# RWKV tile products on all four quarters of the array, the right factor of the inverse as a transpose of the left, and merge's first weights split ahead of its norm

## The reference, cut to what matters

```python
h = rmsnorm(x, p['norm_mix_g'])
u = h @ p['w_in']
o_ssd, ... = ssd_mixer(u_ssd, ...)       # ends with a grouped RMS norm of y
o_rwkv, ... = rwkv_mixer(u_rwkv, ...)
o_mla = attend(...)
gates = jax.nn.sigmoid(h @ p['w_gate'] + p['b_gate'])
merged = gates[0]*(o_ssd @ w_o_ssd) + gates[1]*(o_rwkv @ w_o_rwkv) + gates[2]*(o_mla @ w_o_mla)
x = x + merged @ p['w_out']
```

```python
def step(s, inp):
    r_t, w_t, k_t, v_t, kk_t, a_t = inp
    sa = jnp.einsum('bhvk,bhk->bhv', s, -kk_t)
    s = (s * w_t[:, :, None, :] + sa[..., None] * (kk_t * a_t)[:, :, None, :]
         + v_t[..., None] * k_t[:, :, None, :])
    return s, jnp.einsum('bhvk,bhk->bhv', s, r_t)
```

## Time and profile before

| | us |
|---|---|
| median of 3 executions | 3179.81 |
| lowest and highest of them | 3179.19, 3187.45 |
| the profiled execution | 3192.04 |
| its span in the profile | 3190.2 |
| TensorE busy | 2879.2 (90% of the span) |
| VectorE, ACT, POOL busy | 1796.7, 1349.2, 840.5 |
| stage `rwkv_tiles`, layer 0: first matmul to last DMA issue | 167.5 to 302.43 |
| stage `merge`, layer 0: squares to first unit | 1153.08 to 1169.06 |

### The profile page before, as it was taken

How to read it: one execution, slowest core, us unless ns; L and a number is a source line. 1 busy time by engine, 2 the same in 40 slices (tenths; PEclk the granted TensorE clock), 3 DMA queues, 4 the chain that set the end, 5 groups by cost and what they waited for, 6 DMA issues and landing times. The chain is left out here.

```text
span 3190.2 us, 66465 instructions
## 1 busy us (share of the span) xinstructions
PE 2879.2 (90%) x26560; PEld 2647.9 (83%) x26560; DVE 1796.7 (56%) x3035; ACT 1349.2 (42%) x2168; POOL 840.5 (26%) x696
## 2 busy tenths in 40 slices
PE   7888878999997889999978988789999978898998
PEld 6888547999997769989977984489999976798998
DVE  4843454555655645489448444545566556454893
ACT  4612343544544333254365133444454443333542
POOL 0030000699990400000000300008999804000000
PEclk9999988999998979999989999789999989899999
DMA  5301202212115266365453021022111152664544
GB/s 135 91 5 46 78 10 70 67 40 58 37 34 162 70 165 171 94 176 142 124 120 81 4 75 48 11 75 63 53 48 36 50 157 77 171 166 111 159 138 121
DMA packets 471247, 282.15 MB, mean 88 GB/s; under 512 B 65294, under 2 KB 466488, under 8 KB 470314
## 3 DMA queue, kind: packets, MB, share of 16 engines
q1 hardware_dynamic: 468724, 276.85, 31.4%
q10 hardware_dynamic: 2232, 1.26, 0.2%
HBM read 258.75 MB, written 19.29 MB: 87 GB/s over the span
## 5 line engine op out<-in xcount | busy, mean ns | idle before, releaser
L1112 PE MATMUL key_banks<-w_kb_head,latent_T_head 128*128 128x352 f32 x1536 | 518.4, 337 | 0.0
L1112 PE MATMUL key_banks<-w_kb_rest,latent_T_head 128*128 128x352 f32 x1536 | 496.6, 323 | 0.0
L1112 PE MATMUL key_banks<-w_kb_head,latent_T_rest 128*128 128x352 f32 x1536 | 496.0, 323 | 0.0
L290 DVE TENSOR_TENSOR w_rests<-w_ring,w_heads 128x2048 fp32r<-128x2048 f32 (+1 forms) x152 | 326.2, 2150 | 148.8 <-ACT w_heads L284 148.6
L931 POOL TENSOR_TENSOR rwkv_state_tmp<-rwkv_state,vec 128x1024 f32<-128x1024 f32 x64 | 153.1, 2392 | 683.9 <-DMA rwkv_state<-in_state_rwkv_dram 679.0
L1257 DVE TENSOR_REDUCE w_kb<-key_sq 128x8 f32<-128x1024 f32 x256 | 309.5, 1209 | 0.0
L1172 ACT CAST latent_T_head<-turn_bank 128x256 fp32r<-128x256 f32 x256 | 95.5, 373 | 477.2 <-PE turn_bank L1090 285.0
L284 ACT CAST w_heads<-w_ring 128x2048 fp32r<-128x2048 f32 (+1 forms) x152 | 271.9, 1793 | 51.5 <-ACT conv_last_rows L1795 19.7
L2663 POOL TENSOR_TENSOR L_level<-L,const 128x1024 f32<-128x1024 f32 x24 | 56.0, 2354 | 901.9 <-DVE L L2669 826.5
L1112 PEld LDWEIGHTS key_banks<-w_kb_rest,latent_T_head 128*128 128x128 f32 x1536 | 291.0, 189 | 0.0
L1112 PEld LDWEIGHTS key_banks<-w_kb_head,latent_T_head 128*128 128x128 f32 x1536 | 290.3, 189 | 0.0
(11 more groups left out here) (565 smaller groups left out, 7401.5 us busy)
## 6 DMA issues: line engine op xcount, KB each, us to landing
w_ring<-in_ffn_w_up_dram SPq DMA_DIRECT2D x88, 512.0 KB, 5.1
latents<-in_cache_kv_latent_dram SPq DMA_DIRECT2D x256, 128.0 KB, 2.0
w_ring<-in_w_in_dram SPq DMA_DIRECT2D x52, 512.0 KB, 3.8
w_ring<-in_w_gate_dram SPq DMA_DIRECT2D x48, 512.0 KB, 3.9
w_ring<-in_w_in_dram SPq DMA_DIRECT2D x20, 1024.0 KB, 6.2
w_ring<-in_ffn_w_down_dram SPq DMA_DIRECT2D x32, 384.0 KB, 3.6
w_ring<-in_ffn_w_down_dram SPq DMA_DIRECT2D x32, 320.0 KB, 4.1
rope_keys<-in_cache_k_rope_dram SPq DMA_DIRECT2D x256, 32.0 KB, 1.8
```

Source lines behind the costliest of these rows:

```text
L290: ops.tensor_tensor(rests[:, slot, 0:tiles * P], ring[:, slot, 0:tiles * P], heads[:, slot, 0:tiles * P].bitcast(F32), ALU.subtract).then_ ...
L1112: last = nc.tensor.matmul(kbank[:, 3 * x + n, 0:KB], c[:, x, r * P:(r + 1) * P], w[:, r, cols], start=r == 0 and m == 0, stop=r == 1 and m ...
```

## The change

**In `rwkv_tiles`** the address rules, the order, the inverse and the tail change.

- Quarters: a new `token_half(c, p)` is `p ^ (c & 1)`. Values with tokens on the partitions of an odd chunk are now kept on the other half. A product that goes from features to tokens, or from tokens to features (`to_tokens`, `to_features`, and `by_head(X)` by `by_head(Z)`), reads one half and writes the other where the chunk is odd, so that the 32 matmuls of a group use four quarters of the array in turn (`quads`). A product from tokens to tokens (`in_tokens`: `kav`, the first `z`, `ta`, `tk`) stays on the two quarters that it had, and so do `advance` and the new `from_state`. Of the 62 products of a group, 54 are now on four quarters.
- Inverse: X is no longer updated by Z X and an addition. After each level TensorE turns Y (`const,Y`), and the result is copied into X by VectorE (group 0) and ACT (group 1). POOL's masks no longer wait for X.
- Order: `l` comes first; `bend` and `kend` come ahead of the loop, and `z` and the turn of Y are issued by group.
- Tail: for the chunks 1 and 3 the product of R with the state is a matmul pass of its own (`from_state`), which VectorE adds to the output. The states' bank pair is 6 instead of 4.

**In `merge`** ACT's `w_heads` of units 0 and 1 and `out_heads` of the RWKV branch come ahead of `Ln` and `Exp`, and VectorE's `w_rests` and `out_rests` of the same come ahead of the 8 scalings.

```diff
+                heads_of(0)
+                nc.scalar.copy(oh[:, 0, :, :], branches[0][1][:, :, :]).then_inc(out_rounded, 1)
+                heads_of(1)
...
-                heads_of(0)
-                heads_of(1)
...
+                rests_of(0)
+                dve.wait_ge(out_rounded, 1)
+                nc.vector.tensor_tensor(ol[:, 0, :, :], branches[0][1][:, :, :], oh[:, 0, :, :].bitcast(F32), ALU.subtract).then_inc(out_split, 1)
+                rests_of(1)
...
-                rests_of(0)
-                rests_of(1)
...
-        def both(g):
-
-            for swap in range(2):
-                for t in range(DT):
-                    yield (2 * g + swap, t, 0), (2 * g + 1 - swap, t, 1)
+        st_out, y_added = st.sem("state_stored"), st.sem("y_from_state_added")
+
+        def feature_half(c, p):
+            return p
+
+        def token_half(c, p):
+            return p ^ (c & 1)
+
+        def quads(g):
+
+            for t in range(DT):
+                yield (2 * g, t, 0), (2 * g + 1, t, 0), (2 * g + 1, t, 1), (2 * g, t, 1)
...
         def by_token(buf):
+            return lambda c, t, p: buf[rows(token_half(c, p)), c, t * 64:(t + 1) * 64]
...
+                def multiply(g, slot, lhs, rhs, written):
+                    for quad in quads(g):
+                        for c, t, p in quad:
+                            last = nc.tensor.matmul(out(slot, c, t, written(c, p)), lhs(c, t, p), rhs(c, t, p),
+                                                    start=True, stop=True, skip_group_check=True)
                     return last
...
+                pe.wait_ge(kept["kav"], 2)
+                to_tokens(0, 1, k.kendT, feature_eye).then_inc(made["kend"], 1)
+                pe.wait_ge(kept["bend"], 2)
+                to_tokens(1, 3, k.kendT, feature_eye).then_inc(made["kend"], 1)
+                for g in range(2):
                     pe.wait_ge(level_in, g + 1)
-                    multiply(g, 2 + g, by_token(Ln), eye).then_inc(made["z"], 1)
+                    in_tokens(g, 2 * g, Ln, token_eye).then_inc(made["z"], 1)
                 for n in range(1, 6):
-                    z0 = 0 if n % 2 else 2
                     for g in range(2):
                         pe.wait_ge(level_in, 2 * n + g + 1)
                         pe.wait_ge(kept["y_inv"], 2 * (n - 1) + g + 1)
                         if n == 1:
-                            pe.wait_ge(kept["alpha"], g + 1)
-                        elif g:
-                            pe.wait_ge(kept["x_inv"], 2 * (n - 1) + 1)
-                        multiply(g, z0 + g, by_token(Ln), by_token(Y)).then_inc(made["z"], 1)
+                            pe.wait_ge(kept["kend"], g + 1)
+                        to_features(g, 2 * g + n % 2, Ln, by_token(Y)).then_inc(made["z"], 1)
+                        to_features(g, 2 * g + (n - 1) % 2, Y, token_eye).then_inc(made["x"], 1)
                     for g in range(2):
                         pe.wait_ge(kept["z"], 2 * (n - 1) + g + 1)
-                        pe.wait_ge(kept["x_inv"], 2 * (n - 1) + 2)
-                        pe.wait_ge(kept["y_inv"], 2 * (n - 1) + 2)
-                        slot = z0 if g else 2 - z0
-                        multiply(g, slot, by_token(X), by_token(Z)).then_inc(made["y_inv"], 1)
-                        if n < 5:
-                            if g:
-                                pe.wait_ge(kept["z"], 2 * (n - 1) + 2)
-                            multiply(g, slot + 1, by_token(Z), by_token(X)).then_inc(made["x_inv"], 1)
-                pe.wait_ge(kept["x_inv"], 10)
-                multiply(0, 3, by_feature(k.bendT), eye).then_inc(made["bend"], 1)
-                multiply(1, 1, by_feature(k.bendT), eye).then_inc(made["bend"], 1)
+                        pe.wait_ge(x_kept[g], n)
+                        multiply(g, 2 * g + (n - 1) % 2, by_head(X), by_head(Z), token_half).then_inc(made["y_inv"], 1)
                 for g in range(2):
                     pe.wait_ge(kept["y_inv"], 10 + g + 1)
-                    multiply(g, 2 - 2 * g, by_token(Y), by_token(alpha_tm)).then_inc(made["ta"], 1)
-                    pe.wait_ge(kept["bend"], g + 1)
-                    multiply(g, 3 - 2 * g, by_token(Y), by_token(kav)).then_inc(made["tk"], 1)
-                for g in range(2):
-                    pe.wait_ge(kept["ta"], g + 1)
-                    multiply(g, 2 - 2 * g, by_feature(k.kendT), eye).then_inc(made["kend"], 1)
-                for g in range(2):
-                    pe.wait_ge(kept["tk"], g + 1)
-                    multiply(g, 3 - 2 * g, by_token(TA), by_token(bend_tm)).then_inc(made["g"], 1)
-                for g in range(2):
-                    pe.wait_ge(kept["kend"], g + 1)
-                    multiply(g, 2 - 2 * g, by_token(TA), by_token(BR)).then_inc(made["r"], 1)
-                for g in range(2):
-                    pe.wait_ge(kept["g"], g + 1)
-                    for pair in both(g):
-                        for c, t, p in pair:
-                            nc.tensor.matmul(out(3 - 2 * g, c, t, p), by_token(bend_tm)(c, t, p), by_token(TK)(c, t, p),
+                    in_tokens(g, 2 * g + 1, Y, by_token(alpha_tm)).then_inc(made["ta"], 1)
+                    in_tokens(g, 2 * g, Y, by_token(kav)).then_inc(made["tk"], 1)
...
+                pe.wait_ge(kept["g"], 2)
+                inner(0, 2)
+                pe.wait_ge(kept["h"], 2)
+                from_state(1)
                 pe.wait_ge(kept["s"], 1)
                 advance(2)
+                pe.wait_ge(kept["r"], 2)
+                inner(1, 0)
                 pe.wait_ge(kept["s"], 2)
                 advance(3)
-                outputs(1, 3)
+                from_state(3)
...
```

More of the change, by code:

```diff
@@ L2585, in advance, with inner @@
                             w = slice(t * 64, (t + 1) * 64)
-                            last = nc.tensor.matmul(banks[rows(p), 4 + p, w], G[rows(p), c, w], state(c)[rows(p), w],
+                            last = nc.tensor.matmul(banks[rows(p), 6 + p, w], G[rows(p), c, w], state(c)[rows(p), w],
                                                     start=True, stop=True, skip_group_check=True)
                     last.then_inc(made["s"], 1)
-                def outputs(g, slot):
-                    for pair in both(g):
-                        for c, t, p in pair:
+                def inner(g, slot):
+                    for quad in quads(g):
+                        for c, t, p in quad:
@@ L2598, in outputs @@
-                        for c, t, p in pair:
-                            if c:
-                                last = nc.tensor.matmul(out(slot, c, t, p), by_token(R)(c, t, p), state(c)[rows(p), t * 64:(t + 1) * 64],
+                                                    start=False, stop=c != 2, skip_group_check=True)
+                        for c, t, p in quad:
+                            if c == 2:
+                                last = nc.tensor.matmul(out(slot, c, t, p), by_head(R)(c, t, p), state(c)[rows(p), t * 64:(t + 1) * 64],
@@ L2601, in outputs, with from_state @@
                                                         start=False, stop=True, skip_group_check=True)
                     last.then_inc(made["y"], 1)
+                def from_state(c):
+                    for t in range(DT):
+                        for p in range(2):
+                            w = slice(t * 64, (t + 1) * 64)
+                            last = nc.tensor.matmul(banks[rows(p), 2 + c // 2, w], R[rows(p), c, w], state(c)[rows(p), w],
+                                                    start=True, stop=True, skip_group_check=True)
+                    last.then_inc(made["y_state"], 1)
@@ L2616, in _ @@
                         w = slice(t * 64, (t + 1) * 64)
-                        last = nc.tensor.matmul(banks[rows(p), 4 + p, w], state(CHUNKS)[rows(p), w], eye(0, t, p),
+                        last = nc.tensor.matmul(banks[rows(p), 6 + p, w], state(CHUNKS)[rows(p), w], feature_eye(0, t, p),
                                                 start=True, stop=True, skip_group_check=True)
@@ L2681, in _ @@
-                    nc.vector.tensor_tensor(tiles(X, g), tiles(Ln, g), mask("ident64"), ALU.add).then_inc(kept["x_inv"], 1)
+                    keep("kend", g, kend_tm, 2 * g + 1)
+                for g in range(2):
                     dve.wait_ge(made["z"], g + 1)
-                    nc.vector.tensor_tensor(tiles(Y, g), slot_tiles(2 + g), mask("ident64"), ALU.add).then_inc(kept["y_inv"], 1)
+                    nc.vector.tensor_tensor(tiles(Y, g), slot_tiles(2 * g), mask("ident64"), ALU.add).then_inc(kept["y_inv"], 1)
@@ L2695, in _ @@
                 for g in range(2):
[L2696 to L2697 removed]
+                    keep("tk", g, TK, 2 * g)
                 for g in range(2):
```

151 lines of the change are left out of this document (84 added, 67 removed).

## The result

| | before | changed |
|---|---|---|
| median of 5 executions, us | 3179.81 | 3154.12 |
| lowest and highest | 3172.19, 3187.45 | 3151.44, 3161.64 |
| profiled execution, its span | 3192.04, 3190.2 | 3161.64, 3159.1 |
| ratio with 95% interval | | 0.9909, 0.9888 to 0.993 |

The changed kernel is 26 us faster by the medians and 29 by the ratio (0.8 to 0.9%), where 61 was forecast. Two later measurements put it at 0.4% (see the experiments). The mechanism that was forecast is there. Its size isn't.

The account below looks back on a forecast made before the run. TensorE was taken to bound the RWKV tiles, with instruction delivery as the next limit. Two layers of 22.7 (tiles) and 8.2 us (merge), say 61 less, gave 3119 us against the median 3179.81; range 3068 to 3162.

Parts of the forecast that it names:

- What bounds the kernel: RWKV tiles: TensorE bounds the inverse, busy 78.00 of 78 us in the middle, at full clock.
- the likeliest case: RWKV tiles: instruction delivery paces TensorE, a block in 2.6 to 3.6 us; chance 0.49, range 3098 to 3156.
- Rival 1: RWKV tiles: delivery is hidden and four quarters run at full rate, 110 us less, 3070; chance 0.18.
- The array: RWKV tiles: four quarters at once take 0.93 us per group product; 85 us against 132.4, 47 less per layer.
- rivals 2 and 3: RWKV tiles: quarters don't work at once, 3168, chance 0.12; records have a least distance of 27 ns, 3156, chance 0.05.
- The time per block: RWKV tiles: TensorE gets a block of 256 instructions per 3.0 us, bounds 2.1 and 3.39; 22.7 us less per layer.
- further 5.4 us: RWKV tiles, beyond the blocks: 2.9 for products on two quarters, 1.0 for the cold start, 1.5 for waits in the tail.
- The nearest row: RWKV tiles: the loop's branch shows 3.39 us until TensorE's next instruction, taken as the upper time per block.
- the tiles' 45 us: RWKV tiles: the gain forecast for two layers, 22.7 us less in each.
- Merge: Merge: the first units start earlier after the squares, 8.2 us less per layer, bounds 6.6 and 8.2.
- Rival 4: RWKV tiles: TensorE waits at every block and its clock falls to 1.2 GHz, 25 us more, 3205; chance 0.06.

Follow-up runs that it names:

- the tiles alone: The kernel before with the change of the RWKV tiles alone: 3187.28 us, ratio 0.9996 to before.
- the run on two quarters: The changed kernel with its new order and inverse, but every product on the two diagonal quarters: 3178.19 us, ratio 0.9968 to before.
- the changed kernel's two repeats: The changed kernel again, once as it was and once with register moves that were not in the compiled program: 3170.78 and 3169.81 us, ratios 0.9958 and 0.996.
- the changed kernel padded with waits: The changed kernel with fulfilled waits, one instruction more per quad of matmuls in the products behind l and v: 3201.03 us, ratio 1.0049 to before.
- the three with wide turns: The changed kernel with turns of 64x128, as transposes in two runs and as matmuls by the identity in one: ratios 0.9796, 0.9795 and 0.9854 to before.
- before padded: The kernel before with two fulfilled waits ahead of each pair of matmuls in all products but the first two: 3229.45 us, ratio 1.0135.
- merge alone: The kernel before with the change of merge alone: 3169.94 us, ratio 0.9955 to before.

## Why the prediction was wrong in its size, step by step

- *What bounds the kernel.* Right. The stage was bound by TensorE, and the next limit was the delivery of instructions, as the likeliest case had it: the stops come every 128 records, last 1.36 us in the head of the stage, and have nothing named as releaser. Rival 1 (delivery hidden, 3070) fell: the array reaches 0.93 us per group product and then stands.
- *The array.* Right. Four quarters work at once, 14.4 ns from record to record. That ends rivals 2 and 3.
- *The time per block.* This step failed: "I take 3.0, leaving 0.4 us of the branch to itself". The branch had next to nothing to itself. In it the packet starts 1.0 us after the branch does, takes 1.0 us, and the branch ends 1.4 us behind it (1596.37, 1597.37, 1598.37 and 1599.76 in the trace of before). In the changed kernel it is 1.1, 1.0 and 1.35, 3.45 in all. And 3.45 is the best case, not the mean. In the head of the stage periods of 3.45, 3.73 and 4.0 occur side by side, in the levels others up to 4.1, and the mean is 3.6 in one execution and 3.73 in another. At 3.6 the prediction's blocks alone, 34.75 x 3.6 = 125, are what was measured, 124.7 and 126.4; its further 5.4 us are in part in that mean. With 3.39 it had said 10.8 less per layer, and 8.6 and 6.8 were found. The nearest row was the right one to take.
- *What hung on it.* The two quarters of before need 3.73 us per block. Any delivery near that eats the gain of the quarters whole. So the tiles' 45 us became 15 in the first profile, 7 in that of the tiles alone, and nothing that the comparison of the tiles alone can tell (0.9996).
- *A reading.* The prediction has 132.4 us for the stage before; from the first to the last record it is 133.3, which changes nothing above.
- *Merge.* Right in kind, 8.2 forecast, 5.8 and 7.4 found. The weights of unit 0 were ready 5.8 us after the squares where I had 5.1, and in layer 0 the first half unit ran for a part at half clock (0.64). The kernel before has such a stretch at the same place in both layers; the forecast took it from the time of before and left it out of the time after.
- *The Trainium skill,* "Runtime: NRT & Kernel Launch", section "Instruction fetch mechanics": that crossing a 16 KiB boundary is mostly hidden holds here where the block's work is 3.73 us (no stop in the run on two quarters). Where it is 1.87 us the trace disagrees, with a stop of 1.36 us or more at a block. A store of eight blocks for TensorE doesn't show: the engine stands at each block.
- *Rival 4.* Its 3205 is excluded, but its mechanism is there in small. The first profile has full clock from 207 to 285 at 65% busy. The profiles of the tiles alone, of the changed kernel's two repeats, of the changed kernel padded with waits and two of the three with wide turns have stretches of 3.4 to 10.2 us at half clock inside the stage, behind its start; those of the kernels without long stops (before, before padded, merge alone, two quarters) have none. Where the delivery paces, such a stretch hides in the stops.

What stays open: why one execution has a mean of 3.6 us per block and another 3.73. The packets themselves are a part of it, 1.04 us each on the mean in the stages of the first profile and 1.12 in those of the repeat. The rest is not explained. The chip of the first comparison may be another than that of the repeat, or the steps of some 0.27 us between the periods may be decided by chance.

## What to carry to other kernels

Small float32 matmuls on quarters are dense in instructions: four per matmul, so 64 matmuls are a block of 16 KB, and this straight line of code got a block per 3.45 to 3.75 us on the mean. Before tiles are packed more closely, multiply the stage's blocks by that time and compare with the array's; here the best case stood 0.3 us per block under the array's own, and the mean of two of the profiles at it. From there on what helped was fewer instructions: a wide transpose in one pass in place of matmuls by the identity gave 1.1 to 1.6% over the changed kernel (0.9796 against 0.9909 to 0.996).

## What the runs showed of the hardware that was not expected

- TensorE's instructions come one block of 256 at a time. A straight line of matmuls gets them in periods from 3.45 to 4.1 us, and with fulfilled waits among them in up to 4.6.
- 64x64 float32 matmuls on all four quarters start 14.4 ns apart, half of the 29.2 ns on two.
- 16 transposes of 64x128 take some 0.5 to 0.65 us at full clock, the same turn of Y by matmuls of two passes 1.93.
- A wait that is fulfilled is not free between matmuls on quarters: with two ahead of each pair, a group product went from 1.87 to 2.2 to 2.5 us.
